# Convolution taps in one instruction each, and the norm behind the convolution in two parts

## What is computed

```
h = x @ w_pw1 + b_pw1                          # 1024 -> 2048 channels
h = a * sigmoid(gate)                          # a, gate: the halves of h
h = depthwise_conv(h, w_dw, b_dw)              # 31 taps in time, per channel, padding 15
h = silu(layer_norm(h, g_n, b_n))              # over the channels
mix = h @ w_pw2 + b_pw2
x = layer_norm(ALPHA * x + mix, ...)
```

## Time and profile before

| | us |
|---|---|
| median of three runs | 3003.24 |
| the profiled execution | 3003.5 |
| its span | 3001.1 |
| PE busy | 2876.8 (96%) |
| DVE busy | 1640.7 (55%) |
| POOL busy | 911.8 (30%) |
| ACT busy | 749.3 (25%) |

### The profile page before, as it was taken

One profiled execution on the slowest core, in us unless ns is written; L12 is line 12 of the kernel. 1 busy time (PEld: TensorE's weight loads), 2 busy tenths in 40 slices (PEclk: granted clock), 3 DMA queues, 4 the chain that ended last, 5 costly groups with the idle time before them and its releaser, 6 DMA issues.

```text
span 3001.1 us, 36000 instructions
## 1 busy us (share of the span) xinstructions
PE 2876.8 (96%) x14070; PEld 2347.4 (78%) x14070; DVE 1640.7 (55%) x2612; ACT 749.3 (25%) x1717; POOL 911.8 (30%) x798
## 2 busy tenths in 40 slices
PE   8999959999999999999899899899999999999995
PEld 7888848788888888888788544487888888888884
DVE  3699974744444444444730599727444444444457
ACT  3212343221111111222111466502222111111131
POOL 3354502232233233232132333323223223223323
PEclk9999979999999999999999899999999999999998
DMA  4000003111111111111221000021111111111111
GB/s 131 29 18 25 28 1 119 29 43 31 40 43 39 33 43 43 36 43 36 71 78 32 22 1 1 23 94 36 43 36 40 31 43 43 36 36 43 43 36 70
DMA packets 158644, 124.65 MB, mean 42 GB/s; under 512 B 27905, under 2 KB 135801, under 8 KB 158488
## 3 DMA queue, kind: packets, MB, share of 16 engines
q1 hardware_dynamic: 149640, 96.83, 11.3%
q10 hardware_dynamic: 8848, 25.69, 2.3%
HBM read 112.01 MB, written 10.49 MB: 41 GB/s over the span
## 4 chain that ended last, share of the span: by engine, by line
PE 86%; DVE 9%; ACT 3%; issue 1%; DMA 0%; POOL 0%; POOLq 0%; ACTq 0%; SPq 0%; DVEq 0%
PE bank L588 26%; PE bank L593 26%; PE bank L591 26%; PE bank L953 3%; PE bank L929 2%; DVE conv_acc L1293 2%; PE bank L944 1%; DVE stats L1223 1%; DVE y L1241 1%; DVE x_lo L1249 1%; ACT y L1094 1%; DVE y L1236 1%; DVE y L1451 1%; PE bank L618 1%; ACT probs L1187 1%
## 5 line engine op out<-in xcount | busy, mean ns | idle before, releaser
L588 PE MATMUL bank<-x_hi,w_hi 128*128 128x512 f32 (+1 forms) x2688 | 957.2, 356 | 3.8 <-DVE x_lo L1249 1.6
L591 PE MATMUL bank<-x_lo,w_hi 128*128 128x512 f32 (+1 forms) x2688 | 953.4, 355 | 0.0
L593 PE MATMUL bank<-x_hi,w_lo 128*128 128x512 f32 (+1 forms) x2688 | 953.3, 355 | 0.0
L514 POOL CAST w_hi<-raw_pieces 128x512 fp32r<-128x512 f32 x348 | 329.9, 948 | 1802.9 <-issue 1363.8
L588 PEld LDWEIGHTS bank<-x_hi,w_hi 128*128 128x128 f32 x2688 | 509.5, 190 | 79.0 <-POOL w_lo L518 6.3
L591 PEld LDWEIGHTS bank<-x_lo,w_hi 128*128 128x128 f32 x2688 | 509.5, 190 | 70.6
L593 PEld LDWEIGHTS bank<-x_hi,w_lo 128*128 128x128 f32 x2688 | 509.1, 189 | 70.8
L518 POOL TENSOR_TENSOR w_lo<-raw_pieces,w_hi 128x512 fp32r<-128x512 f32 x348 | 472.2, 1357 | 27.9
L1451 DVE TENSOR_TENSOR y<-y,bank 128x512 f32<-128x512 f32 x440 | 296.2, 684 | 200.5 <-PE bank L593 198.5
L1412 DVE SCALAR_TENSOR_TENSOR gate_conv<-bank,ffn_conv_table,gate_conv 128x510 f32<-128x510 f32 x132 | 86.2, 653 | 373.5 <-ACT up_conv L1125 371.5
L1293 DVE SCALAR_TENSOR_TENSOR conv_acc<-glu,conv_table,conv_acc 128x1024 f32<-128x1024 f32 (+1 forms) x310 | 257.6, 906 | 35.4 <-ACT conv_acc L1034 35.4
(11 more groups left out here) (144 smaller groups left out, 3765.5 us busy)
## 6 DMA issues: line engine op xcount, KB each, us to landing
raw_pieces<-in_ffn_w_up_dram SPq DMA_DIRECT2D x168, 256.0 KB, 2.9
raw_pieces<-in_ffn_w_down_dram SPq DMA_DIRECT2D x84, 256.0 KB, 2.6
raw_pieces<-in_conv_w_pw_dram SPq DMA_DIRECT2D x48, 256.0 KB, 2.7
y<-in_x_prompt_dram ACTq DMA_DIRECT2D x16, 512.0 KB, 6.8
residual_dram<-y ACTq DMA_DIRECT2D x10, 512.0 KB, 2.6
y<-residual_dram ACTq DMA_DIRECT2D x10, 512.0 KB, 10.7
out_dram<-y SPq DMA_DIRECT2D x10, 512.0 KB, 2.6
raw_pieces<-in_attn_w_q_dram SPq DMA_DIRECT2D x32, 128.0 KB, 2.4
```

What stands on the lines that cost most here:

```text
L514: pool.tensor_copy(WH[:, p % RING, :], raw[:, p % RAW, :]).then_inc(piece_hi, 1)
L588: mm = pe.matmul(out, left[0], right[0], start=first, stop=False)
L591: pe.matmul(out, left[0], right[1], start=False, stop=False)
L593: return pe.matmul(out, left[1], right[0], start=False, stop=last)
```

## The change

- Taps: DVE's instruction for a tap now covers the prompt, the gap of 15 columns and the sample in one (1295 columns). It waits for the tap before it. Only the last tap is still two, as it writes to `conv`. PE_TAPS goes from 9 to 8, so DVE has 23 taps.
- Last channel tile: PE takes 26 of its taps (MORE_TAPS 18), DVE 5. DVE no longer adds them to PE's sum moved by ACT: it starts with its own taps and the bias in two column ranges, and then adds PE's PSUM banks (7, 6, 5) chunk by chunk. ACT moves nothing of this tile.
- Norm and SiLU: tiles 0 to 3 go all the way through SiLU and split first. Tiles 4 and 5 are turned before the projection, 6 to 9 between k steps 0 to 3 of block 0. Tiles 4 to 6 are turned back at the end of block 0 and 7 to 9 in block 1. ACT writes SiLU over `conv_normed`; DVE copies the high part itself and then subtracts. Two extra residual steps stand on DVE between these.
- The residual and bias loads move from ACT's queue to SP's, and start when all ten tiles have been turned. Banks are assigned anew.

The core of the diff:

```diff
-    PE_TAPS = 9
-    MORE_TAPS = 13
+    PE_TAPS = 8
+    MORE_TAPS = 18
...
+            def load_residual():
+                sp.wait_ge(silu_lo, EARLY)
+                sp.dma_start(pw2_bias[:], w["conv_b_pw2"][0:1, :].to_broadcast([P, D])).then_inc(bias_landed, 16)
+                sp.wait_ge(ct_turned, TT)
+                for t in range(TT):
+                    sp.dma_start(y[:, t, :], x_rows[t]).then_inc(res_landed[t], 16)
...
+            for t in range(EARLY):
                 back_tile(t)
-            pe.wait_ge(silu_lo, BLOCKS[0][1])
-            out_projection(B_PW2, 0, lambda k: back_tile(BLOCKS[0][1] + k) if BLOCKS[0][1] + k < TT else None)
+            turn_conv_tile(4)
+            turn_conv_tile(5)
+            split_done(EARLY)
+            pe.wait_ge(ct_kept, 2 * EARLY)
+            out_projection(B_PW2, 0, {
+                (0, 0): lambda: turn_conv_tile(6), (0, 1): lambda: turn_conv_tile(7),
+                (0, 2): lambda: turn_conv_tile(8), (0, 3): lambda: turn_conv_tile(9),
+                (0, 6): lambda: back_tile(4), (0, 7): last_of_first_block,
+                (1, 0): lambda: back_tile(7), (1, 1): lambda: back_tile(8), (1, 3): lambda: back_tile(9),
+                (1, 7): lambda: split_done(TT)})
...
+                elif not use and 4 <= t < 8:
+                    pe.wait_ge(proj_kept, t - 3)
...
-                for k in range(taps):
-                    last = k == taps - 1
-                    for c0, n, a0 in ((0, S0, 0), (S0, S1, S0 + PAD)):
...
+                n = S0 + PAD + S1
+                for k in range(taps - 1):
+                    if k > 0:
+                        dve.wait_ge(vec_step, vs.now())
+                    dve.scalar_tensor_tensor(out=acc[:, c, :], in0=glu[:, c, k:k + n], scalar=tap(k),
+                                             in1=acc[:, c, :], op0=ALU.mult, op1=ALU.add
+                                             ).then_inc(vec_step, vs.one())
...
+            def last_channels(a0, n, chunks):
+                tap = lambda k: conv_tab[:, KT - 1, k:k + 1]
+                part = acc[:, 1, a0:a0 + n]
+                dve.tensor_scalar(part, glu[:, 1, a0:a0 + n], tap(0), chan[:, 0, KT - 1:KT], ALU.mult, ALU.add
+                                  ).then_inc(vec_step, vs.one())
...
+            def silu_split(t):
+                dve.wait_ge(silu_ready, t + 1)
+                whole = normed[:, NORMED_AT[t], :].rearrange("p (k t) -> p k t", t=P)
+                dve.tensor_copy(XH[:, :, cols(t)], whole).then_inc(vec_step, vs.one())
+                dve.wait_ge(vec_step, vs.now())
+                dve.tensor_tensor(XL[:, :, cols(t)], whole, XH[:, :, cols(t)].bitcast(F32), ALU.subtract
+                                  ).then_inc(silu_lo, 1)
...
+            for t in range(EARLY):
+                conv_norm(t)
+            for t in range(EARLY - 1):
+                silu_split(t)
+            conv_stats(EARLY)
+            silu_split(EARLY - 1)
+            for t in range(EARLY + 1, TT):
+                conv_stats(t)
+            conv_deviations(1, EARLY, TT)
+            conv_norm(4)
+            conv_norm(5)
+            silu_split(4)
+            conv_norm(6)
+            silu_split(5)
+            add_conv(0)
+            add_conv(1)
+            conv_norm(7)
+            silu_split(6)
+            conv_norm(8)
+            silu_split(7)
+            conv_norm(9)
+            silu_split(8)
+            silu_split(9)
+            for t in range(2, TT):
+                add_conv(t)
```

More of the change, by code:

```diff
@@ L675, in conv_taps @@
                     u = 3 * c + ch
-                    if not first or u >= 2:
+                    out = bank[LAST_BANK[ch] if more else 6 + u % 2]
+                    if more and ch == 2:
+                        pe.wait_ge(sig_ready, i * 6 + 6)
+                    elif not first or u >= 2:
                         pe.wait_ge(acc_ready, i * 6 + u - 1)
@@ L756, in out_projection @@
                             project(base, use, 0, k, t)
[L757 to L760, removed]
+                        between.get((b, k), lambda: None)()
                 for t in range(TT - 2):
@@ L1076, in _, with keep_conv_tile @@
             pw1_round(KT // 2 - 1, False, last=True)
-            for t in range(TT):
+            def keep_conv_tile(t):
                 act.wait_ge(ct_turned, t + 1)
+                if t == EARLY:
+                    act.wait_ge(last_done, 3)
                 for half in range(2):
[L1081 to L1087, removed]
@@ L1089, in _, with conv_deviations, silu_tile @@
-            for t in range(TT):
+                    act.activation(normed[:, NORMED_AT[t], half * HALF:(half + 1) * HALF],
+                                   bank[conv_turn_bank(t) + half][:], ACT.Copy).then_inc(ct_kept, 1)
+            def conv_deviations(t0, t1):
+                act.wait_ge(conv_var, t1)
+                act.activation(std[:, t0:t1], mv[:, t0:t1, 1], ACT.Sqrt, bias=eps[:, 0:1]).then_inc(conv_std, 1)
+            def silu_tile(t):
                 act.wait_ge(cn_turned, t + 1)
-                if t >= 2:
-                    act.wait_ge(silu_lo, t - 1)
@@ L1098, in _ @@
[L1098 to L1104, removed]
+            act.activation(std[:, 0:2], eps[:], ACT.Sqrt)
+            for t0, t1 in ((0, EARLY), (EARLY, TT)):
+                for t in range(t0, t1):
+                    keep_conv_tile(t)
+                conv_deviations(t0, t1)
+                for t in range(t0, t1):
+                    silu_tile(t)
@@ L1105, in _ @@
+            act.wait_ge(silu_lo, TT)
             load_gains(0)
@@ L1286, in conv_taps @@
                 dve.wait_ge(acc_ready, i * 6 + 3 * c + 3)
-                for k in range(taps):
-                    last = k == taps - 1
-                    for c0, n, a0 in ((0, S0, 0), (S0, S1, S0 + PAD)):
[L1290 to L1298, removed]
+                n = S0 + PAD + S1
[5 more added lines that the diff above has]
+                                             ).then_inc(vec_step, vs.one())
                     if k == 3:
                         between()
+                dve.wait_ge(vec_step, vs.now())
+                k = taps - 1
+                for c0, n, a0 in ((0, S0, 0), (S0, S1, S0 + PAD)):
+                    ins = dve.scalar_tensor_tensor(
+                        out=conv[:, bass.ds(i * 2 + c, 1), c0:c0 + n], in0=glu[:, c, a0 + k:a0 + k + n],
+                        scalar=tap(k), in1=acc[:, c, a0:a0 + n], op0=ALU.mult, op1=ALU.add)
                 ins.then_inc(conv_done, 1)
```

176 lines of the change are left out of this document (106 added, 70 removed).

## The result

The changed kernel takes **3017.85 us** (median of 5 runs, 3017.52 to 3019.22); the kernel before, on the same chip, 3002.66 (5 runs, 2999.76 to 3005.05). The ratio is 1.0051, 95% interval 1.0038 to 1.0064: slower by some 15 us, where +4.5 was forecast. The profiled execution took 3017.52 with a span of 3015.0, against 3003.5 and 3001.1, so the two traces differ by 14.0, and it is this difference that can be followed. Of the runs further down, two executions were far off, one of e2_pairs at 3613.90 us and one of e7_static at 10141.66; they are counted in the medians, which they move by under 1 us, and are left out of the ratios.

The account below looks back on a forecast made before the run. PE was taken to bound the kernel (86% of the chain of waits, DVE 9%), with DVE becoming the convolution's bound. Terms +11.1 - 6.6 + 0 = +4.5 on 3003.5 gave 3008.0, as median 3007.7 us; range 2985 to 3016.

Parts of the forecast that it names:

- Step 1: Convolution, merged taps and one moved to DVE: `glu` of half 7 ends at 363.9, before at 352.8; +11.1 us.
- the merged tap: DVE's convolution chains: one merged instruction takes 1.58 to 1.59 us, the pair 1.59, so merging brings nothing.
- POOL's part: POOL's four weight pieces a half get in between merged taps, costing DVE 1.16 us each, 4.65 a half.
- Step 2: Last channel tile: PE's wait of 13.59 us goes, its taps end later, S moves +4.5 against +11.1; -6.6 us.
- S: Start of the last two of PE's first sixteen turned blocks, forecast at 414.8 us, before at 410.24.
- Step 3: Norm, SiLU and projection blocks behind S: front gains given back in four waits; 0, bounds -5 and +5 us.
- the four waits: PE waits before blocks 1 and 2 for residual steps of tiles 0 to 3; block 1 at S + 60.8.
- 1, POOL stays outside: Convolution: POOL is kept out of the merged chain, each half 44.85 us; -0.5 in all, 3002.7; chance 0.15.
- 2, neither counts: Convolution: POOL slips in without further cost to DVE, PE's half of 41.50 holds; -15.3, 2987.9; chance 0.18.
- 3, the merged tap costs less: Convolution: a merged tap takes 1.47 us, one instruction's fixed share less; -10.8, 2992.4; chance 0.10.
- 4, each split in full: Convolution: each piece holds DVE up 1.41 us, half 45.9; +10.4, 3013.6; at 1.9 a piece 3025; chance 0.15.
- 5, longer waits in blocks 0 and 1: Projection: late residual rows or a low clock lengthen these waits, +5 us on any other case; chance 0.07.

Follow-up runs that it names:

- e2_pairs: The changed kernel with two instructions to a tap again (1024 and 256 columns), 8 taps on PE; 3007.84 us, 1.0015 to the kernel before.
- e7_static: The changed kernel, loop kept, each chain first copying its 31 tap values to a fixed address; 3011.6 us, 1.0028 to the kernel before.
- e1_unrolled: The changed kernel with DVE's loop over the convolution rounds written out; 3010.34 us, 1.0024 to the kernel before.
- e3_pairs_pe9: The changed kernel with paired taps and 9 on PE, keeping the last channel tile and new norm order; 2999.91 us, 0.9985 to the kernel before.
- e8_ready_early: e3_pairs_pe9 with residual multiplications of tiles 0, 1 before tile 4's split and 2, 3 before tile 7's; 2994.66 us, 0.997 to the kernel before.
- e6_narrow_splits: The changed kernel with POOL splitting only 8 of 512 columns of weight pieces 8 to 47; 2994.56 us, 0.997 to the kernel before.

## Why the prediction was wrong, step by step

**Step 1, the `glu` of half 7: +11.1 forecast, +16.5 measured (369.33 against 352.80).** This is the step that failed, and in it one term, the merged tap of "1.58 to 1.59, bounds -0.1 and +0.05". That value was near enough in chains 0 and 5, 1.57 + 0.035 = 1.60: their halves came out at 44.98 and 44.75 where 44.93 stood. In chains 1 to 4 it was 1.57 + 0.145 = 1.71, past the upper bound, because I took the restart of a waiting instruction from the earlier trace rows, two instructions whose addresses are fixed, for one whose address a register makes. The pair hid this: in e2_pairs the same register operation stands in the trace too, but while the other instruction of the pair runs. 22 x 0.11 is 2.4 us a half; POOL's part came 1.0 under the forecast there (3.6 against 4.65), so each of the four halves was 1.3 longer, 5.2 in all. The two belong together: a tap beside a subtraction takes 2.37 in the loop and 2.48 outside, one beside a cast 1.69 and 1.80, so the 0.11 does not add where POOL holds the tap up, eight times a half. With the start of chain 0 0.35 later this is the 5.4 missed. e1_unrolled and e7_static each took this gap away by another edit, and the `glu` of half 7 ended 7.4 and 4.4 us earlier; the second pays a copy and its wait in each chain.

What POOL does outside the loop was forecast right, in kind and in size. Timeline of POOL in chain 0 of the changed kernel (before: a cast of 15.96):

```profile
117.58 1.34 POOL L540 CAST w_hi<-raw_pieces 128x512 fp32r<-128x512 f32 x1 [33.76 <-PE bank L614]
119.00 2.43 POOL L544 TENSOR_TENSOR w_lo<-raw_pieces,w_hi 128x512 fp32r<-128x512 f32 x1
121.39 1.88 POOL L540 CAST w_hi<-raw_pieces 128x512 fp32r<-128x512 f32 x1
123.35 2.44 POOL L544 TENSOR_TENSOR w_lo<-raw_pieces,w_hi 128x512 fp32r<-128x512 f32 x1
```

No cast is over 4 us, and one piece goes by in 4.35 us, for which two taps are 2.48 and 1.80 where alone they are 1.57: 1.14 a piece outside the loop, 1.16 forecast.

**Step 2, from there to S: -6.6 forecast, -4.8 measured** (52.6 us in place of 57.4). The early end of chain 7, the gap in front of the taps (3.2, forecast 3.4) and the additions held. The 26 taps took 47.9 (372.56 to 420.42), not 45.8: PE had waited 4.45 and ran the first 5 us at half the clock, eleven products at 0.20 more each, 2.2. e3_pairs_pe9, where PE waits 1.2 there and the clock stays at 1.00, takes 45.7 for them and has -6.7.

**Step 3, behind S: 0 forecast, +2.3 measured.** The first projection product is at S + 25.3 (25.1), so the front half of the plan held to 0.2. Timeline of DVE, then of PE, at the waits before blocks 1 and 2:

```profile
480.73 1.23 DVE L1434 TENSOR_TENSOR x_lo<-conv_normed,x_hi 128x1024 fp32r<-128x1024 f32 x1
481.87 1.22 DVE L1446 SCALAR_TENSOR_TENSOR y<-y,pw_bias_rows 128x1024 f32<-128x1024 f32 x1
483.12 0.69 DVE L1440 TENSOR_TENSOR y<-y,bank 128x512 f32<-128x512 f32 x1
```

```profile
483.92 0.77 PE L614 MATMUL bank<-w_hi,x_hi 128*128 128x512 f32 x1 [3.24 <-issue]
...
485.73 0.79 PE L614 MATMUL bank<-w_hi,x_hi 128*128 128x512 f32 x1 [0.19 <-DVE y L1440]
...
502.76 0.47 PE L614 MATMUL bank<-w_hi,x_hi 128*128 128x512 f32 x1 [1.42 <-issue]
...
504.57 0.50 PE L614 MATMUL bank<-w_hi,x_hi 128*128 128x512 f32 x1 [0.88 <-DVE y L1440]
```

The page's word "issue" is a wait for nothing it can name; the order of DVE's rows names it, as forecast: split, multiplication, addition, then PE. Blocks 1 and 2 start at S + 62.0 and S + 80.8 (60.8 and 78.8). After the wait of 3.24 PE had the low clock again:

```profile
484.00:490.00 6.00, 5.81 (x17) 0.51 0.01 3
```

That was in the bounds of +5, and e8_ready_early shows that DVE's order set most of the four waits: 3.6 of 6.2 us of them went with it. e3_pairs_pe9 lost 4.2 behind S and not 2.3: its block 2 starts 0.5 later, and its clock is low once more from 487.6 to 491.0.

Sum: 16.5 - 4.8 + 2.3 = 14.0, the whole difference of the traces; from the first turn of the second column half on (542.11 against 528.12) the two kernels run alike.

**The rivals.** 1, POOL stays outside: false, by the rows above. 2, neither counts: false; e6_narrow_splits is what it would be with nearly no splits. 3, the merged tap costs less: false, it costs more. (Its sum has a slip: 0.12 x 22 x 6 is 15.8, not 15.3, so its time would be 2991.9.) It went with what the Trainium skill says, that a semaphore after each operation costs nothing ("VectorE: DVE Perf Modes", "The DRAIN you can't avoid") and that one should lower the number of operations and not of semaphores (same page, "Rules for kernel authors"). For a chain in which each instruction waits for the one before, these traces do not agree: half as many instructions took as long, 1.60 against 1.59, with a gap of 0.035 or 0.145 between them against an overlap of 0.08 in the pairs. The Trainium skill's rule that one engine gets the shared port for a whole instruction while the other blocks ("SBUF — State Buffer", "SBUF: two separate sides") agrees with the merged chain, where each split gets in behind the next tap, and not with the first cast beside a paired one (18.75 in e2_pairs). 4, each split in full: its price of 1.41 a piece was not paid (1.14, and 0.9 in the loop), but its time, 3013.6, stood nearest of all; a longer half came about by another way. 5, longer waits in blocks 0 and 1: true by half, +2.3 of +5.

The range (2985 to 3016) ended 1.9 under the median: it held nothing for a merged tap over 1.64, and nothing for the clock after the new waits of PE in front of the last taps.

## What to carry to other kernels

Two chains of instructions that take turns on an engine hide each other's waits. Merging them into one chain, in which each instruction waits for the one before, gives that up: read a restart from rows with the same kind of operand (a fixed address or one from a loop's register), and give a static copy of the scalar its price. An engine that has slack keeps it only so long as the work that shares its port is counted too: here 1.6 us for a tap and 3.6 to 4.7 for four splits, and 2.4 for the addresses in the loop, were all due out of 3 us of DVE's slack. And in an order made to start a stage early, put only the instruction that frees the buffer behind the one that the next stage also needs.

## What the runs showed of the hardware

- An operand address with a loop register in it costs 0.11 us between a wait and the instruction (gap 0.145 against 0.035). This did not show where another instruction of the engine was still running (the paired chain in the loop, e2_pairs: 8 instructions 6.45; the earlier trace rows, outside: 6.46).
- A POOL cast that came in the middle of a chain of DVE's overlapping pairs stood 10.6 to 18.8 us (e2_pairs; 14.2 to 16.2 in the kernel before); beside a chain with gaps of 0.035 or more it took turns with DVE, 0.95 to 1.96 us each. Beside the first pairs of a chain, with POOL's splits already under way, the two took turns as well (e2_pairs, from 179.8 to 187.9).
- Around the PE waits of 4.24, 4.45 and 3.24 us in the changed kernel the granted clock was 0.50 for some 5 us of products (323.5 to 329.4, 372 to 377, 484 to 490). Around shorter ones it went either way: waits of 2.79, 2.79 and 2.78 in e1_unrolled, two with 0.50 (137.9 to 141.3, 226.6 to 230.0) and one with 1.00 (316.4 to 324.0); 2.45 in e8_ready_early with 0.50; two of 1.41 and 0.88 close together with 0.50 in e3_pairs_pe9 (487.6 to 491.0), and two of 1.42 and 0.88 with 1.00 in the changed kernel (502 to 508). In e3_pairs_pe9, where PE waits 1.2 in front of the last taps, it is 1.00 from 357 to 403, and the 26 taps take 45.7 us, not 47.9.
